# The condition's sum over partitions: one product of 192 columns, or four of 48 on four column groups

## What is computed

```python
mod = jax.nn.silu(c) @ w_ada[l] + b_ada[l]          # (1, 1024) @ (1024, 3072) + (3072,)
shift, scale, gate = jnp.split(mod, 3, axis=-1)
h = x * (1.0 + scale[:, None, :]) + shift[:, None, :]
...
x = layer_norm_2(ALPHA * x + (1.0 + gate[:, None, :]) * sub, ln_g[l], ln_b[l])
```

## Time and profile before

| | |
|---|---|
| median of 3 runs | 1355.39 us (1353.21 to 1357.05) |
| the profiled execution | 1354.25 us, its span 1352.4 us |
| granted TensorE clock, mean | 0.997 of full speed |
| PE busy | 1325.5 us, 98% of the span |
| PEld busy | 1122.0 us, 83% |
| VectorE busy | 1003.2 us, 74% |
| ScalarE busy | 661.9 us, 49% |
| GpSimd busy | 105.6 us, 8% |
| moved by DMA | 265.41 MB, 196 GB/s in the mean |

### The profile page before, as it was taken

The page is one execution under the profiler, slowest core; times in us unless marked ns, Lnnn a source line. Parts: engine busy times, 40 slices in busy tenths (PEclk is TensorE's granted clock), DMA queues, the critical chain, the costliest instruction groups (busy, mean ns, idle before and its releaser), DMA issues.

```text
span 1352.4 us, 18605 instructions
## 1 busy us (share of the span) xinstructions
PE 1325.5 (98%) x7172; PEld 1122.0 (83%) x7172; DVE 1003.2 (74%) x1564; ACT 661.9 (49%) x1037; POOL 105.6 (8%) x153
## 2 busy tenths in 40 slices
PE   9999999999999999999999999999999999999997
PEld 7888888787888887888887887888879998799895
DVE  6666678886767776766677886677767789967887
ACT  6444345634444444444437534344446577455681
POOL 1011000011011001111010010111000000000000
PEclk9999999999999999999999999999999999999999
DMA  7966655437667557676556447677568433475430
GB/s 272 332 227 229 226 184 190 125 121 244 233 234 231 183 186 244 229 231 222 194 174 200 126 144 266 236 250 230 167 229 253 158 125 125 140 239 159 151 110 32
DMA packets 179015, 265.41 MB, mean 196 GB/s; under 512 B 16560, under 2 KB 139568, under 8 KB 178416
## 3 DMA queue, kind: packets, MB, share of 16 engines
q1 hardware_dynamic: 167216, 223.63, 50.8%
q0 software_dynamic: 11712, 40.60, 8.4%
HBM read 263.13 MB, written 1.07 MB: 195 GB/s over the span
## 4 chain that ended last, share of the span: by engine, by line
PE 83%; DVE 11%; DMA 3%; issue 1%; ACT 1%; SPq 0%; DVEq 0%; ACTq 0%
PE ps L771 25%; PE ps L773 25%; PE ps L772 25%; DVE w_lo L1243 4%; PE ps L840 3%; DMA w_raw<-in_w_in 2%; PE ps L983 1%; DMA w_raw<-in_ffn_w_gu 1%; DVE few_first L1272 1%; PE ps L1018 1%; DVE arena L1530 1%; PE ps L884 1%; DVE y L1271 1%; ACT w_hi L1074 1%; DVE small L1528 1%
## 5 line engine op out<-in xcount | busy, mean ns | idle before, releaser
L1243 DVE TENSOR_TENSOR w_lo<-w_raw,w_hi 128x1024 fp32r<-128x1024 f32 (+3 forms) x424 | 494.8, 1206 | 191.0 <-ACT w_hi L1074 189.6
L1074 ACT ACTIVATE w_hi<-w_raw 128x1024 fp32r<-128x1024 f32 (+3 forms) x424 | 422.1, 1042 | 295.5 <-DMA w_raw<-in_ffn_w_gu 148.8
L771 PE MATMUL ps<-w_hi,col_hi 128*128 128x512 f32 (+2 forms) x1024 | 400.7, 391 | 10.9 <-DVE col_lo L1254 6.2
L773 PE MATMUL ps<-w_hi,col_lo 128*128 128x512 f32 (+2 forms) x1024 | 391.4, 382 | 0.0
L772 PE MATMUL ps<-w_lo,col_hi 128*128 128x512 f32 (+2 forms) x1024 | 390.9, 382 | 0.0
L771 PEld LDWEIGHTS ps<-w_hi,col_hi 128*128 128x128 f32 x1024 | 192.6, 188 | 51.7 <-DVE w_lo L1243 8.6
L773 PEld LDWEIGHTS ps<-w_hi,col_lo 128*128 128x128 f32 x1024 | 192.4, 188 | 37.5
L772 PEld LDWEIGHTS ps<-w_lo,col_hi 128*128 128x128 f32 x1024 | 192.7, 188 | 33.9
L771 PE MATMUL ps<-w_hi,lat_hi 128*128 128x512 f32 (+2 forms) x544 | 209.0, 384 | 0.2 <-ACT arena L1146 0.2
L773 PE MATMUL ps<-w_hi,lat_lo 128*128 128x512 f32 (+2 forms) x544 | 206.5, 380 | 0.0
L772 PE MATMUL ps<-w_lo,lat_hi 128*128 128x512 f32 (+2 forms) x544 | 206.3, 379 | 0.0
(11 more groups left out here) (143 smaller groups left out, 1154.0 us busy)
## 6 DMA issues: line engine op xcount, KB each, us to landing
w_raw<-in_ffn_w_gu SPq DMA_DIRECT2D x172, 512.0 KB, 5.0
w_raw<-in_w_in SPq DMA_DIRECT2D x54, 1024.0 KB, 5.1
w_raw<-in_ffn_w_down SPq DMA_DIRECT2D x44, 1024.0 KB, 5.2
mod<-in_w_ada POOLq DMA_DIRECT2D x32, 768.0 KB, 7.4
w_raw<-in_w_out SPq DMA_DIRECT2D x12, 1024.0 KB, 4.9
norm_g<-in_ln_g POOLq DMA_DIRECT2D x8, 512.0 KB, 4.0
norm_b<-in_ln_b POOLq DMA_DIRECT2D x8, 512.0 KB, 5.8
w_raw<-in_w_out SPq DMA_DIRECT2D x8, 512.0 KB, 6.3
```

The source lines that it names most:

```text
L771: pe.matmul(dst, a_hi, b_hi, start=start, stop=False)
L773: return pe.matmul(dst, a_lo, b_hi, start=False, stop=stop)
L1074: act.activation(half_of(w_hi[j], n, h), half_of(raw[j], n, h), ACT.Copy).then_inc(hi_ready, 1)
L1243: tt(half_of(w_lo[j], n, h), half_of(raw[j], n, h), half_of(w_hi[j], n, h).bitcast(F32), ALU.subtract)\
```

## The change

The product with ones becomes four, each over 48 of the 192 columns (`MOD_Q`) and with 32 columns of ones as weights. Product g writes partitions 32g to 32g + 31 of the same columns of bank 7, that is on the g-th group of 32 columns of the array. VectorE now copies 128x48 out of PSUM, and the row's four parts stand on partitions 0, 32, 64 and 96, from which the store to DRAM takes them. The bias is added by a VectorE instruction of its own inside `modsum`, on partition 0 of the sum, after its first term; so it passes through the product with ones and arrives in every total. For that, `modsum` waits for the bias, and GpSimd issues the bias load right behind the chunk load, a round earlier than before. Ahead of the copy VectorE waits until the store of the row before has landed.

```diff
+MOD_Q = MOD_W // 4
...
-        ada_row = mod[0:1, (KT + 1) * MOD_W:(KT + 2) * MOD_W]
+        ada_rows = mod[:, (KT + 1) * MOD_W:(KT + 1) * MOD_W + MOD_Q]
...
                     pe.wait_ge(free[b], m)
-                    pe.matmul(bank(7, MOD_W), ones[:, :], ada_sum, start=True, stop=True).then_inc(turned[b], 1)
+                    for g in range(4):
+                        last = pe.matmul(ps[32 * g:32 * g + 32, 7, 0:MOD_Q], ones[:, 0:32], ada_sum[:, g * MOD_Q:(g + 1) * MOD_Q],
+                                         start=True, stop=True)
+                    last.then_inc(turned[b], 1)
...
                     dve.wait_ge(chunk_in, at["chunk_in", job])
+                    dve.wait_ge(bias_in, at["bias_in", job])
                     steps.wait(ts(ada_sum, ada_w[:, 0, :], c_silu[:, 0:1], None, ALU.mult))
+                    steps.wait(tt(ada_sum[0:1, :], ada_sum[0:1, :], ada_bias, ALU.add))
...
                     b, n = TURN["spread", s, job[2]][0]
-                    dve.wait_ge(bias_in, at["bias_in", ("modsum", s, job[2])])
                     dve.wait_ge(turned[b], n + 1)
-                    tt(ada_row, ps[0:1, 7, 0:MOD_W], ada_bias, ALU.add).then_inc(mod_row, 1)
+                    if at["mod_stored", job] > 16:
+                        dve.wait_ge(mod_stored, at["mod_stored", job] - 16)
+                    dve.tensor_copy(ada_rows, ps[:, 7, 0:MOD_Q]).then_inc(mod_row, 1)
...
                         chunk_load(s, c + 1)
+                        bias_load(s, c + 1)
                     pool.wait_ge(mod_row, at["modrow", job])
                     steps.settle()
-                    pool.dma_start(mod_rows[l, cols].partition_broadcast(1), ada_row).then_inc(mod_stored, 16)
+                    pool.dma_start(mod_rows[l, cols].rearrange("(g n) -> g n", g=4), ada_rows[0:P:32, :]).then_inc(mod_stored, 16)
                     pool.wait_ge(mod_stored, at["mod_stored", job])
                     steps.settle()
-                    if c + 1 < MOD_STEPS:
-                        bias_load(s, c + 1)
```

## The result

The changed kernel takes 1357.11 us in the median of 11 runs (1355.69 to 1359.92), the kernel before, beside it, 1353.89 in the median of 11 (1352.3 to 1357.05). The ratio is 1.0025, with a 95% interval from 1.0018 to 1.0033: 3.4 us slower (2.4 to 4.5). The profiled execution has a span of 1356.8 us.

The account below looks back on a forecast made before the run. TensorE (PE), busy throughout the feed-forward stretches, was taken as the bound; 0.34 + 0.10 - 0.34 = +0.10 us a round, +3.2 us over 32 rounds, VectorE and GpSimd covered, forecast 1358.0 us, range 1354.0 to 1364.0.

Parts of the forecast that it names:

- visit: PE, from the transposes' last column to the next large product's first column in a feed-forward round: 0.44 us forecast.
- the product removed: PE, L884 in each feed-forward round: the two-pass f32 product with ones holds the array for 0.34 us.
- switches: PE, around the new products: array empty going to column groups and back, 0.34 us a round.
- products: PE, at L884's place: four products of 48 columns on four groups side by side, 0.10 us a round.
- VectorE, a round: Bias instruction and wait added, copy in place of L1350: +0.2 us a round, hidden by VectorE's idle time, costed at nothing.
- bias landing: GpSimd's bias load, issued behind the chunk load: lands with the chunk, no wait; at worst one VectorE round waits about 1 us.
- The block of L1018: Attention times values, on groups of 64 columns: 0.37 us of its 1.23 are not columns, used to price the switches.
- The rival of two at a time: New products on PE: only two groups run side by side, products take 0.16 us a round, +5.2 us; chance 0.17.
- no overlap at all: New products on PE: eight records one after the other, 0.33 us a round, +10.6 us; chance 0.05.
- The free switch: PE around the new products: the array need not run empty, run falls by 7.7 us; chance 0.08.
- VectorE's cover: Feed-forward rounds: idle time hides VectorE's added 0.2 us; rival that it goes, up to +6 us, chance 0.05.
- The call between "within 0.3%" and "slower": Whole run: chance 0.57 of staying within 0.3% (4.1 us) of no change, 0.35 of slower.

Follow-up runs that it names:

- the detour: Kernel before plus, in every round ahead of L884, one unread product of 16 columns on a group of 32 array columns: 1365.19 us, ratio 1.0075.
- three sizes: 48, 96 and 192 columns per group: the changed kernel, and its variants with two and four chunks a visit; visits of 0.43, 0.51 and 0.67 us.
- the kernel with two groups of 64: The change with two products of 96 columns on two groups of 64 array columns, against the kernel before: 1360.52 us, ratio 1.005.
- the kernel with one group for all four: The change with all four 48-column products on the same group of 32 array columns, against the kernel before: 1365.63 us, ratio 1.0087.
- the one-pass kernel: Sum split into high and low parts, two one-pass products by 96 columns of ones, no groups, against the kernel before: 1349.03 us, ratio 0.9969.
- four chunks: The change with four chunks summed at once, four products of 192 columns every fourth round, against the kernel before: 1350.29 us, ratio 0.9978; again 1350.93, 0.9975.
- the one-pass kernel with two: Split sums of two chunks in two one-pass records of 384 columns every second round, no groups, against the kernel before: 1351.03 us, ratio 0.9973.
- that with one product: All of the change but the four products: one whole-array product of 192 columns, one copy, one store, against the kernel before: 1353.62 us, ratio 1.0.

## Why the prediction was right

It gave +3.2 us, and the ratio makes it +3.4 us; the median of 1357.11 lies in the range and 0.9 below the forecast of 1358.0. That the absolute time came out so near is in part luck: the kernel before took 1353.89 beside it, not the 1355.39 and 1354.25 that the forecast stood on, and the changed kernel's profiled execution is 4.4 us longer than that of before, of which 3.0 are the visits. What was foreseen is the difference and where it arises. Point by point:

| step | forecast | measured |
|---|---|---|
| the product removed | 0.34 us | 0.34, as read from the same rows |
| switches, a round | 0.34 | 0.33 (0.43 less 0.10); 0.32 by the detour in the kernel before |
| products, a round | 0.10 | 0.08 by the slope of three sizes, and 0.02 between the starts of a bunch (3 x 7 ns) |
| visit | 0.44 | 0.43 |
| 32 rounds | +3.2 us | +3.0 by the visits, +3.4 (2.4 to 4.5) by the runs |
| VectorE, a round | +0.35 for the sum, -0.13 for the copy, +0.2 in all, covered | +0.39, -0.13, +0.26 in all, covered |
| bias landing | with the chunk, no wait | the same |

- **Rows of other shapes priced the new ones.** The block of L1018 gave 0.37 us for two switches with 64 columns, and the kernel with two groups of 64 has 0.37 again; 0.03 less for the smaller weight load was in the right direction, and the visit came out 0.01 under the forecast.
- **Four groups at once.** The rows had shown only two. The rival of two at a time (+5.2 us) is refuted by the row of 0.29 us, and no overlap at all (+10.6) is what the kernel with one group for all four costs: 11.8 us by its ratio, 10.2 by its visits. Of the two rules of the Trainium skill that were weighed, both in TensorE: Matmul & The Clock Gate, the one in the section Measured speedup vs the span model, with about 4 ns for each further product of a pack, is the nearer. The other, in the section Wait — 56ns, not 53.3ns?, has record starts never closer than about 25 ns. The rows show eight starts in 0.085 us, 12 ns in the mean and 7 inside a bunch, and the whole is not at the +6.4 us that the second rule would have given.
- **The free switch** fell by the same rows, and by the detour that costs 10 us in the kernel before. The Trainium skill says of it in TensorEngine Tiling (Array Packing), Key Properties, that a change of the tiling mode drains TensorE; the traces agree with it, with 0.32 to 0.33 us for there and back.
- **VectorE's cover** stood with room: the one-pass kernel puts 10 us more on VectorE in a stretch of 160 us, and PE doesn't idle.
- **What was sized too low** is VectorE's part: 0.35 for the bias instruction rather than 0.33, and another 0.05 in the wait behind the copy. Under the cover it didn't matter.
- **The call between "within 0.3%" and "slower"** was close by nature: the interval of the ratio, 1.0018 to 1.0033, touches the bound. The misses of this study are among the expectations. For four chunks, and for the one-pass kernel with two, the PE term came true to 0.01 and 0.02 us and the runs gained 3 to 4 us instead of 5; four products on the whole array lost 20 us instead of 17.

## What to carry to other kernels

In a dense stream of products, going to groups of the array's columns and back costs some 0.35 us here, with 16 as with 192 columns in each group, which is as much as a whole-array product of 200 columns in two passes; split a small product over column groups only where several of them stand together or where the array is grouped already. Before that, look at the format: two one-pass products of a split operand cost less than one two-pass product, if VectorE has room. And price such an edit by what stands on both sides of the product in the trace, not by the product's own records: these went from 0.33 to 0.22 us each and their columns from 0.34 to 0.10 us a round here, and the kernel got slower.

## What was not expected

- **The smallest products aren't the cheapest.** On the whole array, records of 48 columns take 0.11 us each, which goes with their 128 weight columns; cutting one product of 192 columns into four without groups took 20 us.
- **In some executions the granted clock falls once in the second block.** Busy time by stretch; the column ahead of the last two is PEclk. First the kernel before, then the changed one, then the second profile of the kernel before:

```profile
1284.00:1286.00 2.00, 1.07 (x7) 0.84 (x8) 1.97 (x4) 2.00 (x3) 0.00 (x0) 1.00 1.02 420
1286.00:1288.00 2.00, 2.00 (x7) 1.71 (x7) 1.97 (x3) 2.00 (x4) 0.00 (x0) 0.54 0.08 33
```

```profile
1111.00:1113.00 2.00, 1.18 (x7) 0.93 (x8) 1.97 (x4) 2.00 (x3) 0.00 (x0) 1.00 0.99 406
1113.00:1115.00 2.00, 2.00 (x8) 1.72 (x7) 1.97 (x3) 2.00 (x5) 0.00 (x0) 0.53 0.03 10
```

```profile
1286.00:1288.00 2.00, 0.97 (x7) 0.73 (x7) 1.97 (x4) 2.00 (x3) 0.00 (x0) 1.00 1.02 420
1288.00:1290.00 2.00, 2.00 (x14) 1.90 (x15) 1.97 (x3) 2.00 (x3) 0.00 (x0) 1.00 0.06 23
```

All three are the same piece of work, in stage 7 of the kernel before and in stage 6 of the changed one: PE waits for VectorE, 1.1 us in each, and is busy 1.0 to 1.2 of 2 us. In the first two the clock is then granted at 1.2 GHz for most of the next 2 us, and returns to 2.4; in the third it stays at 2.4. So the fall belongs to the execution and not to the kernel: six of the fourteen profiles have one in the second block. It costs 1.6 us in the first profile of before, set record by record against the second, and 1.3 us in the changed kernel, set against that with one product. So it nearly cancels between the first two; but it makes PE of the changed kernel look 6 us late between 1148 and 1284 us, and whoever had compared the two traces there would have doubled the loss.
